# Work orders around the norms and first feed-forward units, one pass for a double norm, a bias by accumulating DMA, and activation tables loaded ahead, in a two-block transformer kernel

## The chip, the cores and the metric

The kernel runs on one core of one Trainium2 chip. The metric is the device time of one execution in microseconds (us); lower is better.

## The reference, cut to what matters

256 tokens of width 1024 pass through two blocks. The first has two layers (a gated linear recurrence, then stick-breaking attention), each followed by a SwiGLU feed-forward, and ends in a norm. The second begins with another norm of that result, so two norms stand back to back.

```python
def rms_norm(x, g):
    return x * lax.rsqrt(jnp.mean(x * x, axis=-1, keepdims=True) + 1e-6) * g

def swiglu_ffn(x, w_in, w_out):                # w_in 1024 x 5632, w_out 2816 x 1024
    gu = x @ w_in
    return (jax.nn.silu(gu[..., :2816]) * gu[..., 2816:]) @ w_out

h = h + rg_lru_block(rms_norm(h, mix_norm[0]), ...)        # ends in y @ w_out + b_out
h = h + swiglu_ffn(rms_norm(h, ffn_norm[0]), ...)
h = h + stick_breaking_attention(rms_norm(h, mix_norm[1]), ...)
h = h + swiglu_ffn(rms_norm(h, ffn_norm[1]), ...)
h = rms_norm(h, final_norm)                                # end of the first block
proj = rmsnorm(h, norm_gain) @ w_in_2                      # start of the second, 24 chunks of 256 columns
# ... q and k head norms, block attention, a gated recurrence, two gated branches, w_out_2, a last gate
```

## The kernel before, in words

**Chunks.** All weights (133 chunks of 128 x 2048 float32, 1 MB each) stream through the core once, in one fixed order. SyncE's queue loads a chunk into one of two `raw` buffers. ScalarE copies it, rounded, to `whi` (L971), VectorE subtracts to get the rest, `wlo` (L1442), and TensorE forms each product as three matmuls (hi by hi, lo by hi, hi by lo; L448 to L457 and L501 to L503). `whi` and `wlo` are rings of four chunks. `split(c)` converts chunk c; it waits for the chunk to land and for TensorE to be done with chunk c - 4. `ahead(c)` is `split(c + 3)`. The load of chunk c + 2 waits for VectorE's half of `split(c)`, so a late split makes the load after next late.

**Order.** There is no scheduler. Each engine runs the list of instructions that its block of the program writes out, in that order, and the engines meet at semaphores. A piece of work that waits holds up everything behind it on its engine.

**Stages.** `STAGES` names them: `rec_a` to `branch_b` and `lru_out` (recurrence), `ffn_in0`, `ffn_out0`, `qkv`, `attn_out`, `ffn_in1`, `ffn_out1`, `mix_in`, `up_a`, `up_b`, `out2`, `ple`, `ple_gate`. At each `..._out` stage the residual `h` is updated half by half (`residual`, L1512). TensorE transposes it (`transposes`, L510; its second half in `late_transposes`), ScalarE multiplies the gain in and rounds to `xhi` (`norm_hi`, L997), VectorE makes `xlo` (`norm_lo`, L1469). The norm's factor is not needed for that: ScalarE squares and sums (`norm_square`, L1007), VectorE adds (`norm_sum`, L1478), ScalarE takes the root (`norm_root`, L1013), VectorE the reciprocal (`norm_factor`, L1485), and the factor is applied to products. For stages whose columns are tokens it goes through `diag` (L1495) and TensorE's `factor_rows` (L518).

**Feed-forward.** A unit is 256 of the 2816 hidden columns, two chunks (inner halves r = 0, 1). When a unit is complete ScalarE takes the sigmoid (L1187), VectorE gates it (`gated`, L1771 and L1776), TensorE transposes it (`gate_transposes`, L649), ScalarE and VectorE split it (`gate_hi`, `gate_lo`). The units stand in 4 banks, two to a unit.

**Attention.** For each of four head groups: `logits`, ScalarE's `log_terms` (exp, then ln), `fail_hi`, VectorE's `neg_log_fail`, TensorE's `suffixes` (L731 and after), `exponents`, `weights` (exp, L1229), `weighted_values`, `outputs`.

**Double norm.** After `ffn_out1` VectorE multiplies `h` by the first factor and the final gain (L1902), ScalarE squares the product (L1341), and `both_factors` gives the factor of both. The head norms of `mix_in` (`head_square`, `head_root`, `head_norm`) and the block attention follow.

**Output bias.** SyncE's queue loads it to all partitions (`bout`), and GpSimd adds it to `h` (L426).

**Tables.** ScalarE's functions come from table sets. Where the next function lies in another set, an ACT_TABLE_LOAD stands in its list.

## Time and profile before

| what | value |
|---|---|
| time, median of 3 runs | 925.23 us (924.8 to 925.44) |
| the profiled execution: its time, and its span | 928.87 us, 927.1 us |
| mean granted clock of TensorE | 0.971 |
| TensorE busy | 855.6 us, 92% |
| VectorE busy | 586.7 us, 63% |
| ScalarE busy | 484.6 us, 52% |
| DMA | 146.17 MB, mean 158 GB/s |

The time is that of the whole execution; the span runs from the first to the last instruction of the profile. A busy TensorE at a granted clock of 0.5 is busy without doing as much as it could, so its idle time and its clock are to be read together.

### The profile page before, as it was taken

The page shows a single profiled execution, that of the slowest core. Times are in us where ns is not written, and L with a number is a line of the kernel's source. Part 1 is how long each engine was busy: PE and PEld are TensorE (multiplying, and loading weights), DVE is VectorE, ACT ScalarE, POOL GpSimd, SP SyncE. Part 2 cuts the span into 40 slices and gives each one's busy share as a digit, 9 for nine tenths or more (in the row PEclk, how much of TensorE's full clock was granted, in tenths as well). Part 3 has the DMA queues.
Part 4 walks back from the last instruction along what each step waited for, and adds up shares of the span by engine and source line. Part 5 has one row for each costly group of instructions (what it writes and reads, how often), then busy time and mean ns, then how long its engine had stood idle before and what let it go on. Part 6 is the DMA issues. An engine that isn't in the chain of part 4 may idle for free.

```text
span 927.1 us, 12198 instructions
## 1 busy us (share of the span) xinstructions
PE 855.6 (92%) x5089; PEld 754.2 (81%) x5089; DVE 586.7 (63%) x703; ACT 484.6 (52%) x555; POOL 18.7 (2%) x14
## 2 busy tenths in 40 slices
PE   4897597999999998999898999999998999999998
PEld 4897475888888898998676888888887999999986
DVE  5788945666653556666436655645465588987864
ACT  5678436444443437676355444443357764557432
POOL 3012000000000000000000000000000000000000
PEclk9899698999999998999999999999999999999999
DMA  8454335655555534444436555556444435443451
GB/s 291 135 171 136 107 120 164 197 184 182 182 182 193 192 116 139 133 137 136 136 109 187 182 182 182 184 196 208 138 144 156 142 106 169 150 136 137 137 182 46
DMA packets 120207, 146.17 MB, mean 158 GB/s; under 512 B 3272, under 2 KB 96984, under 8 KB 120024
## 3 DMA queue, kind: packets, MB, share of 16 engines
q1 hardware_dynamic: 118952, 143.80, 48.0%
q10 hardware_dynamic: 1200, 1.59, 0.5%
q8 instruction: 40, 0.66, 0.3%
q14 instruction: 15, 0.12, 0.0%
HBM read 144.32 MB, written 1.06 MB: 157 GB/s over the span
## 4 chain that ended last, share of the span: by engine, by line
PE 70%; DVE 11%; ACT 11%; DMA 5%; issue 3%; SPq 0%; ACTq 0%; DVEq 0%
PE bank L501 16%; PE bank L503 15%; PE bank L502 15%; DVE wlo L1442 5%; PE bank L448 5%; PE bank L449 5%; PE bank L450 5%; ACT whi L971 4%; DMA raw<-in_lru_w_in 2%; PE bank L854 2%; DMA raw<-in_w_in 1%; PE bank L649 1%; DMA raw<-in_ffn_w_in 1%; PE bank L510 1%; DVE a_rc L1619 1%
## 5 line engine op out<-in xcount | busy, mean ns | idle before, releaser
L1442 DVE TENSOR_TENSOR wlo<-raw,whi 128x2048 fp32r<-128x2048 f32 x133 | 304.7, 2293 | 144.0 <-ACT whi L971 143.7
L971 ACT ACTIVATE whi<-raw 128x2048 fp32r<-128x2048 f32 x133 | 253.4, 1910 | 135.7 <-PE bank L503 44.3
L448 PE MATMUL bank<-xhi,whi 128*128 128x256 f32 x576 | 166.8, 290 | 8.7 <-DVE wlo L1442 5.0
L449 PE MATMUL bank<-xlo,whi 128*128 128x256 f32 x576 | 164.5, 286 | 0.0
L450 PE MATMUL bank<-xhi,wlo 128*128 128x256 f32 x576 | 164.2, 285 | 0.0
L501 PE MATMUL bank<-whi,xhi 128*128 128x512 f32 x384 | 153.6, 400 | 3.8 <-DVE xlo L1469 3.0
L503 PE MATMUL bank<-whi,xlo 128*128 128x512 f32 x384 | 150.7, 392 | 0.0
L502 PE MATMUL bank<-wlo,xhi 128*128 128x512 f32 x384 | 150.6, 392 | 0.0
L448 PEld LDWEIGHTS bank<-xhi,whi 128*128 128x128 f32 x576 | 111.8, 194 | 10.8 <-issue 6.2
L449 PEld LDWEIGHTS bank<-xlo,whi 128*128 128x128 f32 x576 | 112.0, 194 | 0.1
L450 PEld LDWEIGHTS bank<-xhi,wlo 128*128 128x128 f32 x576 | 111.9, 194 | 0.0
L501 PEld LDWEIGHTS bank<-whi,xhi 128*128 128x128 f32 x384 | 73.0, 190 | 19.7 <-issue 5.3
L503 PEld LDWEIGHTS bank<-whi,xlo 128*128 128x128 f32 x384 | 72.8, 190 | 15.7
L502 PEld LDWEIGHTS bank<-wlo,xhi 128*128 128x128 f32 x384 | 72.9, 190 | 14.7 <-issue 0.2
L501 PE MATMUL bank<-whi,a_ghi 128*128 128x512 f32 x176 | 68.9, 391 | 0.0
L503 PE MATMUL bank<-whi,a_glo 128*128 128x512 f32 x176 | 68.5, 389 | 0.0
L502 PE MATMUL bank<-wlo,a_ghi 128*128 128x512 f32 x176 | 68.5, 389 | 0.0
L1187 ACT ACTIVATE a_sg<-bank,stat 128x256 f32<-128x256 f32 x44 | 18.4, 470 | 61.4 <-PE bank L503 61.4
L1168 ACT ACTIVATE a_ghi<-bank 128x512 fp32r<-128x512 f32 x22 | 13.2, 598 | 66.7 <-PE bank L649 66.7
L503 PEld LDWEIGHTS bank<-whi,a_glo 128*128 128x128 f32 x176 | 33.0, 188 | 6.9
L502 PEld LDWEIGHTS bank<-wlo,a_ghi 128*128 128x128 f32 x176 | 33.1, 188 | 6.8
L501 PEld LDWEIGHTS bank<-whi,a_ghi 128*128 128x128 f32 x176 | 33.0, 188 | 6.7
(315 smaller groups left out, 1278.6 us busy)
## 6 DMA issues: line engine op xcount, KB each, us to landing
raw<-in_ffn_w_in SPq DMA_DIRECT2D x88, 512.0 KB, 4.7
raw<-in_w_in SPq DMA_DIRECT2D x24, 1024.0 KB, 5.2
raw<-in_ffn_w_out SPq DMA_DIRECT2D x20, 1024.0 KB, 5.1
raw<-in_attn_w_qkv SPq DMA_DIRECT2D x12, 1024.0 KB, 5.1
raw<-in_lru_w_in SPq DMA_DIRECT2D x8, 1024.0 KB, 6.2
raw<-in_lru_w_out SPq DMA_DIRECT2D x4, 1024.0 KB, 5.2
raw<-in_attn_w_o SPq DMA_DIRECT2D x4, 1024.0 KB, 5.2
raw<-in_w_out SPq DMA_DIRECT2D x4, 1024.0 KB, 5.0
```

What stands on the lines that cost most here:

```text
L448: nc.tensor.matmul(dst, wh, hi, start=start, stop=False, skip_group_check=shared)
L449: nc.tensor.matmul(dst, wh, lo, start=False, stop=False, skip_group_check=shared)
L450: return nc.tensor.matmul(dst, wl, hi, start=False, stop=stop, skip_group_check=shared)
L501: nc.tensor.matmul(dst, hi, wh, start=start, stop=False)
L502: nc.tensor.matmul(dst, hi, wl, start=False, stop=False)
L503: return nc.tensor.matmul(dst, lo, wh, start=False, stop=stop)
L510: last = nc.tensor.transpose(bank[X_BANKS[j]][:, m * S + a * P:m * S + (a + 1) * P], h[:, a, f0:f0 + P], ident)
L854: last = nc.tensor.matmul(dst, k[:, u * P:(u + 1) * P], queries, start=True, stop=True)
L971: nc.scalar.activation(whi[:, c % RING, :], raw[:, c % RAWS, :], ACT.Copy)\
L1168: nc.scalar.activation(ghi[:, q, :], bank[G_BANKS[q % 2]][:, :], ACT.Copy).then_inc(g_hi, 1)
L1187: nc.scalar.activation(sg[:, q % 2, a, :], bank[(b0 + 2 * q + a) % 4][:, 0:S], ACT.Sigmoid, scale=stat[:, 10 * xn + 8 + a:10 * xn + 9 + a] ...
L1442: nc.vector.tensor_tensor(wlo[:, c % RING, :], raw[:, c % RAWS, :], whi[:, c % RING, :].bitcast(F32), ALU.subtract).then_inc(lo_dve, 1)
```

## The change

The feed-forward's chunks are taken in another order for the first two units, the splits and the norm's steps are written elsewhere in the lists, the two norms after `ffn_out1` take their sums of squares in one pass from `h` and from `hg` (`h` times the final gain), the output bias is added by a DMA, and table sets are loaded by an explicit instruction at chosen places.

```diff
+IN_ORDER = OUT_ORDER + tuple((q, r) for q in range(2, FFN_PAIRS) for r in range(2))
+def unit_end(q):
+    return 2 if q == 0 else 2 * q + 1
...
-            sp.dma_start(bout[:, :], bass.AP(t["lru_b_out"].tensor, 0, [[0, P], [1, D]])).then_inc(s_bout, 16)
...
             def output_bias():
-                pool.wait_ge(s_bout, 16)
                 pool.wait_ge(sq_ready, 4)
+                pool.wait_ge(chunk_done, 4)
                 for a in range(2):
-                    nc.gpsimd.tensor_tensor(h[:, a, :], h[:, a, :], bout[:, :], ALU.add).then_inc(bout_in, 1)
+                    nc.gpsimd.dma_start(h[:, a, :], bass.AP(t["lru_b_out"].tensor, 0, [[0, P], [1, D]]),
+                                        accum_op=ALU.add).then_inc(bout_in, 16)
... TensorE, outputs_wide (lru_out, attn_out, out2)
                 part(2, 0, 2)
-                part(3, 0, 2)
+                part(3, 0, 1)
                 if second:
                     second()
+                part(3, 1, 2)
                 part(2, 2, 4)
... TensorE, ffn: over IN_ORDER; p is the chunk's place in ffn_in
+                    if p == 0:
+                        late_transposes(xn, ready, count)
+                    if layer and p == 2:
                         relative_bias()
+                    if p == 4:
+                        gate_transposes(layer, 0)
+                    if p > 4 and p % 2:
+                        gate_transposes(layer, p // 2 - 1)
... TensorE, first_two (qkv, mix_in)
                 columns_part(c0, b0, xhi, xlo, 0, 4, x_lo, 4 * xn)
+                late_transposes(xn, acc_read, 2 * xn)
                 columns_part(c0 + 1, b0 + 1, xhi, xlo, 0, 4, x_lo, 4 * xn)
-                late_transposes(xn, acc_read, 2 * xn)
... TensorE, mix_in
-                2: [lambda: factor_rows(5, 2)],
+                1: [lambda: factor_rows(2)],
... ScalarE
+            nc.scalar.preload_act_table_set("sqrt_and_others")      # the list's first instruction
...
-            def norm_wide(xn, b0):
-                for j in range(4):
-                    norm_hi(xn, j)
-                for c in range(2):
-                    act.wait_ge(banks_read, b0 + 2 * c + 2 + 4)
-                    norm_square(xn, c)
-            norm_wide(1, b0)
-            ahead(c0 + 3)
+            def norm_wide(xn, c0, b0):
+                ahead(c0 + 3)
+                norm_hi(xn, 0)
+                norm_hi(xn, 1)
+                act.wait_ge(banks_read, b0 + 2 + 4)
+                norm_square(xn, 0)
+                act.wait_ge(banks_read, b0 + 4 + 4)
+                norm_square(xn, 1)
+                norm_hi(xn, 2)
+                norm_hi(xn, 3)
... ScalarE, ffn_in
+                for p in range(2 * FFN_PAIRS):
+                    if p == 1:
+                        norm_root(xn)
+                    if p == 3:
+                        sigmoids(0)
+                    if p > 3 and p % 2 == 0:
+                        sigmoids(p // 2 - 1)
+                    split(c0 + p + AHEAD)
... ScalarE, end of ffn_out
-                norm_hi(xn + 1, 2)
-                norm_hi(xn + 1, 3)
                 act.wait_ge(acc_read, 4 * layer + 4)
-                norm_square(xn + 1, 1)
+                if layer:
+                    norm_squares_two(1)
+                    act.wait_ge(ms_ready, 5)
+                    nc.scalar.activation(two[:, :, 6:8], two[:, :, 4:6], ACT.Sqrt, scale=1.0 / D)...
+                else:
+                    norm_square(2, 1)
+                    norm_root(2)
+                nc.scalar.preload_act_table_set("natural_log_exp_and_others")
+                norm_hi(xn + 1, 2)
+                norm_hi(xn + 1, 3)
... ScalarE, attention's last group
             fail_hi(GROUPS - 1)
+            ahead(STAGES["attn_out"][0] + 1)
             weights(GROUPS - 1)
... VectorE, norm_wide; the aheads before it stand before its call
-                ahead(c0 + 1)
-                ahead(c0 + 2)
                 residual_wide(name, 0)
+                ahead(c0 + 3)
                 norm_lo(xn, 0)
                 norm_lo(xn, 1)
                 residual_wide(name, 1)
+                norm_sum(xn)
                 norm_lo(xn, 2)
                 norm_lo(xn, 3)
-                norm_sum(xn)
-                ahead(c0 + 3)
... VectorE, double norm
+                def final_gain(c):
+                    cols = slice(c * WIDE, (c + 1) * WIDE)
+                    for a in range(2):
+                        dve.wait_ge(acc_read, 4 * layer + 2 * c + a + 1)
+                        nc.vector.tensor_tensor(hg[:, a, cols], h[:, a, cols], fgain[:, cols], ALU.mult)...
-                nc.vector.scalar_tensor_tensor(out=h[:, a, :], in0=h[:, a, :], scalar=tok(4, a), in1=fgain[:, :], ...)
+            def final_norm():                                       # in mix_in, c == 5
+                dve.wait_ge(xt_mm, 16)
+                for a in range(2):
+                    nc.vector.tensor_scalar(h[:, a, :], hg[:, a, :], tok(4, a), None, ALU.mult)...
... VectorE, attention's last group
             neg_log_fail(GROUPS - 1)
+            ahead(c0a + 1)
             exponents(GROUPS - 1)
             outputs(GROUPS - 1)
+            ahead(c0a + 2)
```

**Order, VectorE, from the first half of `lru_out`'s residual into `ffn_in0`.** Before, the residual and both pairs of `xlo` come first, and the next split (`wlo`) after them; `a_gt` is the first gated unit.

```order
L1512 TENSOR_TENSOR h<-bank,h 128x512 x2
L1469 SCALAR_TENSOR_TENSOR xlo<-bank,par,xhi 128x256 x4
L1512 TENSOR_TENSOR h<-bank,h 128x512 x2
L1469 SCALAR_TENSOR_TENSOR xlo<-bank,par,xhi 128x256 x4
L1478 TENSOR_TENSOR stat<-stat 128x2
L1442 TENSOR_TENSOR wlo<-raw,whi 128x2048
L1485 RECIPROCAL stat<-stat 128x2
L1442 TENSOR_TENSOR wlo<-raw,whi 128x2048 x2
L1771 SCALAR_TENSOR_TENSOR a_gt<-bank,stat,a_sg 128x256 x2
```

The same place in the changed kernel:

```order
L1548 TENSOR_TENSOR h<-bank,h 128x512 x2
L1478 TENSOR_TENSOR wlo<-raw,whi 128x2048
L1505 SCALAR_TENSOR_TENSOR xlo<-bank,par,xhi 128x256 x4
L1548 TENSOR_TENSOR h<-bank,h 128x512 x2
L1514 TENSOR_TENSOR stat<-stat 128x2
L1505 SCALAR_TENSOR_TENSOR xlo<-bank,par,xhi 128x256 x4
L1478 TENSOR_TENSOR wlo<-raw,whi 128x2048
L1521 RECIPROCAL stat<-stat 128x2
L1478 TENSOR_TENSOR wlo<-raw,whi 128x2048 x2
L1805 SCALAR_TENSOR_TENSOR a_gt<-bank,stat,a_sg 128x256 x2
```

One split (chunk 2 of `ffn_in0`) has moved ahead of the first `xlo`, and four of them instead of three stand ahead of the first gated unit. `attn_out` and `ffn_in1` are written in the same way.

**Order, ScalarE, from the last squares of `ffn_out0` into `qkv` and the first group's `log_terms`.** Before:

```order
L997 ACTIVATE xhi<-bank,par 128x256 x4
L1007 ACTIVATE sq,stat<-h 128x512 x2
L1013 ACT_TABLE_LOAD
L1013 ACTIVATE stat<-stat,small 128x2
L971 ACTIVATE whi<-raw 128x2048
L1246 ACTIVATE a_suffix_r<-const 128x256
L971 ACTIVATE whi<-raw 128x2048 x3
L1215 ACTIVATE a_ee<-a_zz 128x1536
L1216 ACT_TABLE_LOAD
L1216 ACTIVATE a_ee<-a_ee 128x1536
L1219 ACT_TABLE_LOAD
```

In the changed kernel, where no table load follows in the attention stage:

```order
L1017 ACTIVATE sq,stat<-h 128x512 x2
L1029 ACTIVATE stat<-stat,small 128x2
L1244 ACT_TABLE_LOAD
L1006 ACTIVATE xhi<-bank,par 128x256 x4
L980 ACTIVATE whi<-raw 128x2048
L1290 ACTIVATE a_suffix_r<-const 128x256
```

The squares, the root and the table load now come ahead of the second half's `xhi`, and the load of the root's table is gone from here (it stands early in `ffn_out0`).

**Order, ScalarE, from the last `xhi` after `ffn_out1` to the head norms of `mix_in`.** Before:

```order
L1013 ACT_TABLE_LOAD
L1013 ACTIVATE stat<-stat,small 128x2
L1341 ACTIVATE sq,stat<-h 128x1024 x2
L1344 ACTIVATE stat<-stat,small 128x2
L971 ACTIVATE whi<-raw 128x2048 x2
L1277 ACTIVATE a_e_even<-a_mq 128x1024
L971 ACTIVATE whi<-raw 128x2048 x2
L1277 ACTIVATE a_qe<-a_mk 128x1024
L1284 ACT_TABLE_LOAD
L1284 ACTIVATE a_e_even<-bank,small 128x512 x2
L1287 ACT_TABLE_LOAD
L1287 ACTIVATE a_e_even<-a_e_even 128x1024
```

In the changed kernel:

```order
L1017 ACTIVATE sq,stat<-h 128x512 x2
L1017 ACTIVATE sq,stat<-a_hg 128x512 x2
L1239 ACTIVATE stat<-stat 128x2x2
L1244 ACT_TABLE_LOAD
L1006 ACTIVATE xhi<-bank,small 128x256 x4
L980 ACTIVATE whi<-raw 128x2048 x3
L1320 ACTIVATE a_e_even<-a_mq 128x1024
L980 ACTIVATE whi<-raw 128x2048 x2
L1320 ACTIVATE a_qe<-a_mk 128x1024
L1327 ACTIVATE a_e_even<-bank,small 128x512 x2
L1330 ACTIVATE a_e_even<-a_e_even 128x1024
```

The squares of both norms and one root for both stand ahead of the last `xhi`, and the table loads of the head norms are gone. Over its whole list ScalarE has 37 table loads before and 23 in the changed kernel.

## Rows read from the trace of the kernel before

**Rows 1.** The page: busy us (share of the span) and instructions by engine

```profile
PE 855.6 (92%) x5089; PEld 754.2 (81%) x5089; DVE 586.7 (63%) x703; ACT 484.6 (52%) x555; POOL 18.7 (2%) x14
```

**Rows 2.** Waits of TensorE: waiting <- releaser, total us, times, longest us

```profile
PE bank L501 <- DVE a_ylo L1692: 15.9, 2, 8.4
PE bank L649 <- DVE a_gt L1776: 9.9, 2, 5.4
...
PE bank L803 <- DVE a_mk L1932: 3.5, 1, 3.5
...
PE bank L518 <- DVE diag L1495: 3.3, 2, 1.9
...
PE bank L510 <- DVE h L1512: 3.1, 1, 3.1
PE bank L501 <- DVE xlo L1469: 3.0, 2, 1.5
PE bank L448 <- DVE xlo L1469: 2.8, 2, 1.4
```

**Rows 3.** Busy us by stretch; after POOL: granted clock, DMA share, GB/s

```profile
156.40:160.40 4.00, 3.97 (x12) 3.31 (x13) 2.89 (x2) 0.70 (x3) 0.00 (x0) 0.50 0.86 266
...
365.10:372.20 7.10, 7.09 (x34) 7.10 (x35) 6.58 (x7) 4.84 (x3) 0.00 (x0) 0.52 0.25 76
...
460.70:464.90 4.20, 4.15 (x16) 3.42 (x17) 0.88 (x2) 0.88 (x3) 0.00 (x0) 0.59 1.04 345
...
491.80:495.20 3.40, 3.37 (x10) 2.89 (x11) 2.89 (x2) 2.18 (x3) 0.00 (x0) 0.51 0.48 168
...
716.50:720.40 3.90, 3.85 (x21) 3.54 (x22) 3.90 (x11) 0.00 (x0) 0.00 (x0) 0.56 0.80 266
14.00:23.00 9.00, 7.39 (x49) 7.22 (x49) 8.56 (x10) 5.20 (x10) 6.83 (x2) 1.00 0.96 327
...
685.40:690.90 5.50, 5.50 (x49) 5.50 (x48) 4.87 (x5) 4.64 (x3) 0.00 (x0) 1.00 0.52 177
```

**Rows 4.** Timeline, `lru_out` into `ffn_in0`: start, us, engine, [idle before <- releaser]

```profile
126.99 1.29 DVE L1512 TENSOR_TENSOR h<-bank,h 128x512 f32<-128x512 f32 x2 [3.04 <-PE bank L503]
129.90 0.88 DVE L1469 SCALAR_TENSOR_TENSOR xlo<-bank,par,xhi 128x256 fp32r<-128x256 f32 x2 [1.62 <-ACT xhi L997]
142.95 2.29 DVE L1442 TENSOR_TENSOR wlo<-raw,whi 128x2048 fp32r<-128x2048 f32 x1 [1.64 <-ACT whi L971]
150.57 1.91 ACT L971 ACTIVATE whi<-raw 128x2048 fp32r<-128x2048 f32 x1 [4.24 <-DMA raw<-in_ffn_w_in]
```

**Rows 5.** Timeline, ScalarE and TensorE, `ffn_out0` into `qkv`

```profile
334.26 1.57 ACT L997 ACTIVATE xhi<-bank,par 128x256 fp32r<-128x256 f32 x4 [9.10 <-PE bank L510]
338.56 1.90 ACT L971 ACTIVATE whi<-raw 128x2048 fp32r<-128x2048 f32 x1
349.08 1.91 ACT L971 ACTIVATE whi<-raw 128x2048 fp32r<-128x2048 f32 x1 [6.51 <-DMA raw<-in_attn_w_qkv]
357.50 1.28 ACT L1216 ACT_TABLE_LOAD   x1
365.11 0.36 PE L731 MATMUL bank<-a_nlhi,a_suffix_r 128*128 128x256 f32 x1 [3.52 <-DVE a_nllo L1837]
```

**Rows 6.** Timeline, VectorE and TensorE in `attn_out`

```profile
453.29 0.50 PE L501 MATMUL bank<-whi,a_ohi 128*128 128x512 f32 x1 [1.41 <-DVE a_olo L1849]
455.00 4.49 DVE L1442 TENSOR_TENSOR wlo<-raw,whi 128x2048 fp32r<-128x2048 f32 x2 [1.76 <-ACT whi L971]
```

**Rows 7.** Timeline, ScalarE and VectorE, `ffn_out1` into `mix_in`

```profile
670.68 0.64 ACT L1007 ACTIVATE sq<-h 128x512 f32<-128x512 f32 x1
675.66 2.48 DVE L1902 SCALAR_TENSOR_TENSOR h<-h,stat,a_fgain 128x1024 f32<-128x1024 f32 x2
```

**Rows 8.** The chain that ended last, at the start: start us, us, what

```profile
14.09 8.70 DMA raw<-in_lru_w_in
```

More of the change, by code:

```diff
@@ L154, in over @@
             return nc.alloc_sbuf_tensor_at("a_" + name, shape, dt, offset=base + int(kb * 1024))
-        bout = over("bout", 0, [P, D])
         prow = over("prow", 17, [P, 2, P])
@@ L180, in build @@
         fgain = over("fgain", 70, [P, D])
+        hg = over("hg", 62, [P, 2, D])
         qa = over("qa", 0, [P, 2, 2, S])
@@ new lines, in ffn @@
+                for p, (q, r) in enumerate(IN_ORDER):
+                    chunk_ready(None, c0 + p)
+                    if r == 0:
+                        for a in range(2):
+                            pe.wait_ge(banks_read, b0 + 2 * q + a + 1)
+                    for k in range(4):
+                        kk = 4 * r + k
+                        if q == 0 and k % 2 == 0:
+                            pe.wait_ge(x_lo, 4 * xn + kk // 2 + 1)
+                        for a in range(2):
+                            last = product_wide(bank[(b0 + 2 * q + a) % 4][:, :], (c0 + p) % RING, k,
+                                                xhi[:, kk, a * P:(a + 1) * P], xlo[:, kk, a * P:(a + 1) * P],
+                                                kk == 0, kk == DT - 1)
+                    last.then_inc(chunk_done, 1)
+                    if p == 0:
+                        late_transposes(xn, ready, count)
+                    if layer and p == 2:
+                        relative_bias()
+                    if layer and p == 4:
+                        pe.wait_ge(bias_read, 4)
+                    if p == 4:
+                        gate_transposes(layer, 0)
+                    if p > 4 and p % 2:
+                        gate_transposes(layer, p // 2 - 1)
@@ L1164, in ffn, with sigmoids @@
                 c0, _, b0 = STAGES[f"ffn_in{layer}"]
[L1166 to L1181 removed]
+                def sigmoids(q):
+                    act.wait_ge(chunk_done, c0 + unit_end(q) + 5)
                     if q == 0:
@@ L1188, in ffn, with gate_hi @@
                                              scale=stat[:, 10 * xn + 8 + a:10 * xn + 9 + a]).then_inc(sig_ready, 1)
-                c0 = STAGES[f"ffn_out{layer}"][0]
+                def gate_hi(q):
+                    act.wait_ge(gt_mm, FFN_PAIRS * layer + q + 1)
+                    nc.scalar.activation(ghi[:, q, :], bank[G_BANKS[q % 2]][:, :], ACT.Copy).then_inc(g_hi, 1)
+                for p in range(2 * FFN_PAIRS):
[6 more added lines that the diff above has]
+                    split(c0 + p + AHEAD)
+                    if layer and p == 3:
+                        for n in range(4):
+                            act.wait_ge(bias_mm, n + 1)
+                            nc.scalar.activation(pair(bias, n), bank[4 + n][:, :], ACT.Copy)\
+                                .then_inc(bias_read, 1)
+                    if p == 5:
+                        gate_hi(0)
+                    if p > 5 and p % 2 == 0:
+                        gate_hi(p // 2 - 2)
+                c0o = STAGES[f"ffn_out{layer}"][0]
                 for c in range(FFN_PAIRS):
-                    split(c0 + c + AHEAD)
                     if c == 0:
+                        sigmoids(FFN_PAIRS - 1)
+                    split(c0o + c + AHEAD)
+                    if c == 0:
+                        gate_hi(FFN_PAIRS - 2)
+                        nc.scalar.preload_act_table_set("sqrt_and_others")
+                    if c == 2:
                         gate_hi(FFN_PAIRS - 1)
@@ L1523, in norm_wide @@
                 c0 = STAGES[name][0]
-                ahead(c0 + 1)
-                ahead(c0 + 2)
                 residual_wide(name, 0)
+                ahead(c0 + 3)
                 norm_lo(xn, 0)
@@ L1755, in _ @@
             output_lo(3)
-            dve.wait_ge(bout_in, 2)
+            ahead(STAGES["lru_out"][0] + 1)
+            ahead(STAGES["lru_out"][0] + 2)
+            dve.wait_ge(bout_in, 32)
             norm_wide("lru_out", 1)
```

178 lines of the change are left out of this document (82 added, 96 removed).

## The prediction

> **What bounds the kernel now.** I read the page first: TensorE is busy 92% of the span, every other engine 63% or less [rows 1]. So a saving counts only where TensorE waits, or runs at its lower clock. I then read TensorE's waits by releaser [rows 2], the granted clock by stretch [rows 3], and the timeline around each wait [rows 4 to 7]. A chunk takes TensorE 5.5 us (48 matmuls of 256 columns, or 24 of 512; 49 of the first kind stand in the row from 685.40 [rows 3]). The steady stages have no waits; the waits stand where one stage hands over to the next. Where TensorE had stood for more than 3 us the clock was granted at 0.50 to 0.59 for the next 3.4 to 7.1 us, that is, mostly at 1.2 GHz instead of 2.4. After the wait of 1.9 us for `diag` it stayed at 1.00 [rows 2, 3]. A slow stretch costs its length times one minus the clock: 2.0 us (156.4), 3.4 (365.1), 1.7 (460.7), 1.7 (491.8), 1.7 (716.5).
>
> **The change part by part.** The 15.9 us that TensorE waits for `a_ylo` [rows 2] lie in the recurrence, whose lists stay as they are; they are only shifted.
>
> *A, `lru_out` into `ffn_in0`.* Lost now: 5.4 (`a_gt`), 1.5 (`xlo`, the longest of two) and the clock's 2.0, together 8.9 us [rows 2, 3]. Why: chunk 2's split stands after all `xlo` work, so VectorE's half runs at 142.95 to 145.24; the load that it lets go lands at 150.57, 5.3 us later; only behind that chunk's split comes the first unit's gate [rows 4]. In the changed order this split can begin once TensorE is done with `lru_out` chunk 2, at 126.99, where the residual begins [rows 4]. Its load was let go late too, and I place its landing about 1 us behind that. Then 1.9 and 2.3 us of conversion end at 132.2, 13 us earlier than now. The price: the first `xlo` pair is behind it on VectorE and ends 0.9 later, at 133.1, where it now ends at 130.8 [rows 4]. TensorE waits for it: 2.2 us. Behind its late transposes TensorE now finds a chunk that needs only the first half's `xlo`, 5.5 us of work, so the 1.5 us go. Following the lists on: chunk 5's load lands near 150, its split and the sigmoid's table end near 154.5, the gate near 156.1; TensorE wants the banks for chunk 4 at 155.9: 0.3 us. What used to hide the gate (one chunk) is now almost two. Remaining 2.5, gain **6.4**.
>
> *B, `ffn_out0` into `qkv`.* Lost: 1.4 (`xlo`), 3.5 (`a_nllo`) and the clock's 3.4: 8.3 us [rows 2, 3, 5]. The late transposes move 2.8 us forward, behind 24 matmuls instead of 48, and half a chunk of the second column group then covers their conversion. Squares, root and table load (1.3 us) use the time in which ScalarE now idles (9.1 us before 334.26). So chunk 3's split starts near 334.3 instead of 338.56, the load that follows lands about 5 us before 349.08, and `log_terms` loses two table loads of 1.28 us each [rows 5]. `a_nllo` is then ready some 6 us or more sooner, against a wait of 3.5 and TensorE arriving 1.4 sooner. Nothing is left of it: gain **8.3**. The loads taken out in later head groups are worth nothing: TensorE's matmuls cover ScalarE there.
>
> *C, `attn_out` into `ffn_in1`.* Lost: 1.4 (`a_olo`), 3.1 (`h`), 1.7, 1.5, 4.5 (`a_gt`) and 1.7: 13.9 us [rows 2, 3, 6]. Moving the weighted values up by 6 matmuls (1.4 us) covers `a_olo` to 0.2. The wait for `h` is VectorE's two splits from 455.00, 4.49 us ahead of the residual [rows 6]; one is now done before `exponents`, in idle time. The other still waits for ScalarE, behind its two DMA issues. I get the residual 2.0 us after TensorE asks for it: less than 3.1, and short enough to keep the clock. Then `xlo` behind a split, 0.4 (the residual was late anyway). The gate is hidden as in A, and `relative_bias` adds cover. Remaining 2.6, gain **11.3**.
>
> *D, `ffn_out1` into `mix_in`.* Lost: 1.4 (`xlo`), 1.9 (`diag`), 3.5 (`a_mk`), 1.7: 8.5 us [rows 2, 3]. Added: four products `hg` at 0.65 us each on VectorE (as L1512) and four squares on ScalarE (0.64 each) instead of two long ones; taken off: 2.48 us of scaling `h` ahead of a split [rows 4, 7]. Half of the added work lies inside `ffn_out1`, in idle time. The other half stands between the last residual and `xlo`: 1.3 + 1.3 (products, then the second pair of squares) + about 0.8 of sums and root + 1.3 of table load (B's duration) + `xhi` and `xlo` put `xlo` some 8 us behind TensorE's last chunk, the residual's 1.3 ahead of it included; TensorE has 2.8 + 0.8 + 2.8 us of other work until then. It waits 1.5 us, as now. `diag` is early, and the four table loads of the head norms (5.1 us) plus the split that starts 5 us sooner bring `a_mk` in time. What comes late next is the first block attention's `a_probs`: ScalarE's split of the chunk ahead used to fit into the wait for `a_mk`, now it is due after it, and `moba_max`, exponentials, the next split and `moba_scale` follow in a row: I get 2.3 us of new wait. Remaining 3.8, gain **4.7**.
>
> *E, the start.* The chain runs through a load of 1 MB that takes 8.70 us to land [rows 8], in a stretch where the DMA engines are at share 0.96 and 327 GB/s [rows 3]; split, parameters, convolution and the recurrence follow from its landing. Removed: the bias's 0.5 MB in front of it, 1.6 us at that rate. Added at about 16 us: two DMAs of 0.5 MB, 3.2 us at that rate if they are served ahead of it. No row shows an accumulating DMA. Lower end: they come behind, 1.6 us gained. Upper end: each costs double, as it reads what it adds to, 4.8 us lost. I take all of it ahead at the plain rate, the nearest row: **1.6 lost**. The two table loads taken off ScalarE at the start gain nothing, it waits for that landing anyway.
>
> Sum: 6.4 + 8.3 + 11.3 + 4.7 - 1.6 = 29.1 us. The profiled execution took 928.87 us (span 927.1), 3.6 above the median of 925.23. 928.87 - 29.1 = 899.8; against the median, **896**.
>
> **The rivals.**
>
> *R1, loads are the bound where conversions were.* For: A and C rest on loads landing in 5.3 us, while the one at the start takes 8.70 [rows 8], and at 460.7 the engines are at share 1.04 [rows 3]. Against: the steady stages ask for a chunk every 5.5 us, at a share near 0.5 (0.52 in the row from 685.40 [rows 3]). If two loads of each entry land 3 us late, the gate is too, TensorE stands 3.3 us and the clock falls: (3 + 1.8) x 2, about 10 us back: 906.
>
> *R2, no new waits.* The accumulation comes behind the load (E +1.6 instead of -1.6), and the probabilities are in time: 896 - 3.2 - 2.3, about 890. For: no row shows when GpSimd's DMAs begin to move bytes. Against: a share of 0.96 leaves no room beside the load [rows 3]. The Trainium skill ("DMA: Bandwidth & Descriptors", SWDGE vs HWDGE vs iDMA) says that an accumulating DMA is issued by GpSimd alone and that each engine takes turns between its internal queues. By that rule it doesn't queue behind the load but halves its pace, which is E's loss and against R2; no run here shows it yet.
>
> *R3, the double norm gives nothing.* If ScalarE's two squares, root and table load ahead of `xhi` are later than I make them, TensorE waits more than 3 us at 670 and the clock falls: D's 4.7 go, 901.
>
> *R4, slower than before.* VectorE waits for both accumulations before the first residual at 126.99 [rows 4]. They are issued near 16. To undo 29.1 us and pass 0.2% they must land after about 158 us, 1 MB in 142 us or 7 GB/s, against 327 [rows 3]. Nothing in the rows comes near that.
>
> *R5, no change*: the waits return one stage later, each for the same time. For: a split made early frees nothing if the chunk after it is as late as before. Against: in A, 13 us are gained for a wait of 5.4.
>
> **How the numbers follow.** Forecast (890 to 902) 0.52; R1 0.17; R2 with the faster side of the forecast's unknowns 0.16; R3 0.10; R4 0.03; R5 0.02. The range takes in R1, R2 and R3 and E's bounds (893 and 899): 885 to 906. A difference under 0.2%, 1.9 us, can't be told from no change. Faster 0.95, same 0.02, slower 0.03. The likeliest is 896.
>
> **What would show it.** A: `wlo` of chunk 2 near 130 to 132, a wait of about 2 us for the first `xlo`, none over 1 us for `a_gt`. B: none for `a_nllo`. C: a wait for `h` of about 2 us. D: none for `diag` and `a_mk`, about 1.5 for `xlo`, about 2 for `a_probs`. E: the load of rows 8 landing at 24.4. A mean granted clock above 0.971. The prediction is wrong if waits over 3 us with a low clock behind them stand in the feed-forward entries, or if the start is more than 5 us later.

## The result, and the profile after

The changed kernel takes 894.57 us (median of 4 runs, 893.75 to 897.05), the kernel before 925.01 us beside it. The ratio is 0.9676, with a 95% interval of 0.9656 to 0.9697: 3.2% faster, 30 us. The profiled execution took 894.26 us, its span is 892.5, its mean granted clock 0.982. Forecast were 896 us, with a range of 885 to 906.

The page, busy time by engine, beside [rows 1]:

```profile
PE 842.4 (94%) x5089; PEld 744.5 (83%) x5089; DVE 582.6 (65%) x707; ACT 467.0 (52%) x544; POOL 13.8 (2%) x14
```

TensorE does the same 5089 matmuls in 13 us less of busy time. Fewer of them run at the lower clock: the mean granted clock rose from 0.971 to 0.982. The other 21 us between the two traces are idle time. Its waits, beside [rows 2]:

```profile
PE bank L509 <- DVE a_ylo L1724: 15.5, 2, 8.0
PE bank L456 <- DVE a_rclo L1665: 6.9, 2, 6.1
PE bank L821 <- DVE a_probs L2020: 2.6, 1, 2.6
PE bank L456 <- DVE xlo L1505: 2.3, 1, 2.3
PE bank L509 <- DVE xlo L1505: 2.3, 2, 1.7
PE bank L729 <- DVE a_olo L1923: 2.0, 3, 0.7
PE bank L518 <- DVE h L1548: 0.9, 1, 0.9
```

The waits for `a_gt` (9.9 us), `a_nllo` (3.5), `a_mk` (3.5) and `diag` (3.3) are gone. What is left of the handovers is short: `xlo` three times, `h` once, and a wait for `a_probs` of 2.6 us that was 1.3 before. The wait for `a_rclo`, in the recurrence whose lists were not touched, grew from 3.9 to 6.9 us. It moves by itself: the longer of its two waits is 3.7 to 6.1 us in the ten traces here that have the bias DMAs where the change puts them. And the stretch around it is no longer than before.

**Where the time went, by stage.** One event is taken as a mark in each trace: the first residual of `lru_out`, `ffn_out0`, `ffn_out1` and `out2` on VectorE, and the wait for `a_olo` of the third head group on TensorE. In the timeline of the changed kernel (start, us, engine, what) they are:

```profile
126.91 1.29 DVE L1548 TENSOR_TENSOR h<-bank,h 128x512 f32<-128x512 f32 x2 [3.84 <-PE bank L511]
296.17 0.68 DVE L1548 TENSOR_TENSOR h<-bank,h 128x512 f32<-128x512 f32 x1
413.56 0.48 PE L729 MATMUL bank<-a_qa,a_ka 64*128 64x256 f32 x1 [0.66 <-DVE a_olo L1923]
610.16 0.68 DVE L1548 TENSOR_TENSOR h<-bank,h 128x512 f32<-128x512 f32 x1
855.62 0.69 DVE L1548 TENSOR_TENSOR h<-bank,h 128x512 f32<-128x512 f32 x1 [0.38 <-PE bank L511]
```

In the kernel before the same five stand at 126.99 [rows 4], 304.16, 430.14, 639.14 and 890.25. The kernel before was also profiled once more (see the first experiment); its marks are 126.79, 303.85, 429.84, 638.67 and 887.76. Differences of neighbouring marks, in us:

| stretch (part of the prediction) | before | before, again | changed | gain | forecast |
|---|---|---|---|---|---|
| start to `lru_out` (E) | 126.99 | 126.79 | 126.91 | 0 | -1.6 |
| to `ffn_out0` (A) | 177.17 | 177.06 | 169.26 | 7.9, 7.8 | 6.4 |
| to the third head group (B) | 125.98 | 125.99 | 117.39 | 8.6 | 8.3 |
| to `ffn_out1` (C) | 209.00 | 208.83 | 196.60 | 12.4, 12.2 | 11.3 |
| to `out2` (D) | 251.11 | 249.09 | 245.46 | 5.7, 3.6 | 4.7 |
| to the end | 36.85 | 36.84 | 36.88 | 0 | 0 |
| span | 927.1 | 924.6 | 892.5 | 34.6, 32.1 | 29.1 |

In the two traces of the kernel before, the stretches outside the start and D repeat to 0.2 us. In the kernels run below, those that have the same lists in a stretch repeat to 0.1 us in B, in C and at the end. They do not in A (169.26 to 171.42 in four kernels) and not in D (244.65 to 247.03 in nine). A is not independent of the start: in those four kernels the first mark stands between 124.73 and 126.91, the second between 295.77 and 296.17, so A takes back what the start gains. Start and A are best read as one sum; for it the forecast was 4.8 and the gain 8.0 and 7.7.

Two places in detail. `lru_out` into `ffn_in0`, VectorE and ScalarE of the changed kernel, beside [rows 4]:

```profile
129.17 2.29 DVE L1478 TENSOR_TENSOR wlo<-raw,whi 128x2048 fp32r<-128x2048 f32 x1 [0.97 <-ACT whi L980]
131.38 1.65 DVE L1505 SCALAR_TENSOR_TENSOR xlo<-bank,par,xhi 128x256 fp32r<-128x256 f32 x4
149.84 1.92 ACT L980 ACTIVATE whi<-raw 128x2048 fp32r<-128x2048 f32 x1 [4.45 <-DMA raw<-in_ffn_w_in]
153.06 0.84 ACT L1193 ACTIVATE a_sg<-bank,stat 128x256 f32<-128x256 f32 x2
```

The first sigmoid in the kernel before:

```profile
153.79 0.84 ACT L1187 ACTIVATE a_sg<-bank,stat 128x256 f32<-128x256 f32 x2
```

Chunk 2's `wlo` is at 129.17, 13.8 us earlier than the 142.95 of [rows 4]. The split behind which the first sigmoid stands is at 149.84 against 150.57 there; it is that of chunk 5 now and was that of chunk 4. The first sigmoid is at 153.06 against 153.79. The split of chunk 2 came 13.8 us sooner, the first gate 0.7. That asks for an experiment. `ffn_out1` into `mix_in`, ScalarE and VectorE of the changed kernel, beside [rows 7]:

```profile
639.59 0.21 ACT L1239 ACTIVATE stat<-stat 128x4 f32<-128x4 f32 x1 [0.63 <-DVE stat L1828]
639.82 1.28 ACT L1244 ACT_TABLE_LOAD   x1
641.98 1.66 DVE L1505 SCALAR_TENSOR_TENSOR xlo<-bank,small,xhi 128x256 fp32r<-128x256 f32 x4 [1.46 <-ACT xhi L1006]
```

The four squares, the root and the table load stand ahead of the last `xhi`, and TensorE waits 2.3 us for the `xlo` behind them (forecast: 1.5).

### The profile page after: what moved, and what is told of

Same layout as the page of the kernel before. It is cut to its first block, busy times and chain, and to the rows that moved or that the text cites. A ratio compares the mean times of both kernels' runs of the same rounds, so it can differ in the third digit from the quotient of the medians.

```text
span 892.5 us, 12188 instructions
## 1 busy us (share of the span) xinstructions
PE 842.4 (94%) x5089; PEld 744.5 (83%) x5089; DVE 582.6 (65%) x707; ACT 467.0 (52%) x544; POOL 13.8 (2%) x14
## 4 chain that ended last, share of the span: by engine, by line
PE 76%; DVE 9%; ACT 8%; DMA 4%; issue 3%; SPq 0%; ACTq 0%; DVEq 0%
PE bank L509 15%; PE bank L511 15%; PE bank L510 15%; PE bank L456 6%; PE bank L457 6%; PE bank L458 6%; DVE wlo L1478 4%; ACT whi L980 4%; PE bank L463 2%; PE bank L464 2%; PE bank L465 2%; PE bank L863 2%; DMA raw<-in_ffn_w_in 1%; DMA raw<-in_lru_gate_w 1%; PE bank L658 1%
## 5 line engine op out<-in xcount | busy, mean ns | idle before, releaser
L1805 DVE SCALAR_TENSOR_TENSOR a_gt<-bank,stat,a_sg 128x256 f32<-128x256 f32 x44 | 19.3, 480 | 28.4 <-ACT a_sg L1193 28.4
```

The source lines that it names most:

```text
L1805: marks.append(mark(nc.vector.scalar_tensor_tensor(out=gt[:, q % 2, a, :], in0=bank[(b0 + 2 * q + a) % 4][:, 0:S], scalar=tok(xn, a), in1= ...
```

## Experiments

All ratios are to the kernel before, run on the same chip in the same session (its medians: 926.14 us for the bias and `e_split_late`, 925.87 for `e_gate_late`, `e_gate_early`, `f_mid` and `f_best`, 926.72 for the others). The changed kernel was not run again beside them; its ratio is 0.9676 (0.9656 to 0.9697), from its own session.

### The kernel before, profiled again

> The kernel before, unchanged, profiled once more. Its profiled execution took 928.87 us against a median of 925.23, and my trace differences of 34.6 us start from there, while the medians differ by 30.4. If the 3.6 us are a scatter of single executions, this one comes within 1 us of 925 and its trace shows where they lay. If profiling itself costs the kernel before 3.6 us (and the changed kernel nothing: 894.26 against a median of 894.57), it comes at 928 to 929 again.

It took 926.41 us, span 924.6. Profiling does not cost 3.6 us; the profiled execution that stood at the base of the prediction had a span longer by 2.5 us, 2.0 of it in D (251.11 against 249.09 in the table). There a load of `mix_in` landed later, and TensorE's clock was 0.56 behind the wait for `a_mk` [rows 3]. In the second trace that wait was 3.2 us, and the clock behind it stayed at 1.00:

```profile
714.60:718.60 4.00, 3.98 (x35) 3.83 (x36) 4.00 (x11) 0.00 (x0) 0.00 (x0) 1.00 0.81 260
```

### The output bias: back on SyncE's queue, or let go later

```diff
# e_bias_old
+            sp.dma_start(bout[:, :], bass.AP(t["lru_b_out"].tensor, 0, [[0, P], [1, D]])).then_inc(s_bout, 16)
...
-                    nc.gpsimd.dma_start(h[:, a, :], ..., accum_op=ALU.add).then_inc(bout_in, 16)
+                    nc.gpsimd.tensor_tensor(h[:, a, :], h[:, a, :], bout[:, :], ALU.add).then_inc(bout_in, 1)
# e_bias_late
-                pool.wait_ge(chunk_done, 4)
+                pool.wait_ge(rc_ready, 1)
```

> The changed kernel with the output bias as before: a load of 0.5 MB to all partitions on SyncE's queue ahead of the constants, and GpSimd's add. The prediction has the accumulating DMAs cost 1.6 us net (3.2 of DMA time ahead of the 1 MB load against 1.6 saved), so this would come 1.6 us faster, at 893.0. The trace of the changed kernel speaks against it: its start is 0.8 us earlier than in the trace before, so the rival expects this kernel 0.5 to 1.5 us slower, 895 to 896, with the 1 MB load landing near 22.8 us again instead of 21.7. If the first matmuls of the gates depend on neither, within 0.5 us.

895.28 us (5 runs), ratio 0.9663 (0.9650 to 0.9676).

> The changed kernel with its two accumulating DMAs let go only when the recurrence stage is under way (near 39 us) instead of at 16 us. If they take DMA time from the load of the gates' weights, which lands at 31.3 us in the changed kernel and on which ScalarE waits 1.15 us, that load lands about 3 us earlier and the kernel is 1.1 us faster (893.5), the most that the chain at the start gives before ScalarE's own work is the bound. Rival, the DMAs cost nothing where they are: no change, within 0.4 us. A third way, that the transfer let go at 39 us now collides with the chunk loads of the recurrence: up to 1 us slower.

895.17 us (4 runs), ratio 0.9661 (0.9647 to 0.9674). Neither differs from the changed kernel's 0.9676. The chain of the changed kernel at the start:

```profile
2.61 7.95 DMA raw<-in_lru_w_in
20.95 10.36 DMA raw<-in_lru_gate_w
```

The load of [rows 8] is no longer in the chain: ScalarE splits that chunk at 21.73 instead of 22.81. The next load does carry the accumulation (10.36 us, ScalarE waits 1.15 us for it), and let go late it doesn't: that split starts at 28.92 instead of 31.32. In the kernel with the late DMAs:

```profile
28.92 1.90 ACT L980 ACTIVATE whi<-raw 128x2048 fp32r<-128x2048 f32 x1
```

So the accumulating DMAs share the engines with a load, as the Trainium skill has it ("DMA: Bandwidth & Descriptors", SWDGE vs HWDGE vs iDMA), but mainly with the load after the one that I had named. What it costs can't be seen at the next mark: the first residual stood at 124.7 with the late DMAs, at 126.4 with the old way, and between 124.6 and 126.9 in ten executions that have the DMAs where the change puts them. The start scatters by 2.3 us, more than the whole of E. At an earlier point the order is clear in every trace. The first long wait for `a_ylo` ends at 94.70 and 94.74 in the kernel before and at 94.40 with the bias in the old way. With the DMAs where the change puts them it ends between 92.88 and 93.99 (ten traces), and with the late DMAs at 92.40. By these traces the DMAs gain 0.4 us or more there against the old way (one trace, and the two of the kernel before), and late ones somewhat more (one trace); neither shows in the total time.

### One piece undone at a time: the early split, the order of chunks

```diff
# e_split_late (ScalarE; VectorE alike), in norm_wide
-                ahead(c0 + 3)
                 norm_hi(xn, 0)
...
                 norm_hi(xn, 3)
+                ahead(c0 + 3)
# e_order_old
-IN_ORDER = OUT_ORDER + tuple((q, r) for q in range(2, FFN_PAIRS) for r in range(2))
+IN_ORDER = tuple((q, r) for q in range(FFN_PAIRS) for r in range(2))
```

> The changed kernel with one piece undone: in lru_out and attn_out the split of chunk 2 of the following feed-forward stands behind all of the norm's work again, on ScalarE and VectorE, while the order of the chunks stays changed. By the prediction's reason for parts A and C (the early split is what makes the first gated unit early; chunk 2's wlo at 145 instead of 131), waits for a_gt of 3 us and more with a low clock behind them come back in both feed-forward entries: 4 to 6 us each, 902 to 906. Rival: the order of chunks alone hides the gate, and the early split only makes the first xlo late (1.7 and 0.6 us of wait): then this kernel is within 1 us, or up to 2 us faster.

897.86 us (4 runs), ratio 0.9693 (0.9677 to 0.9708). This interval overlaps that of the changed kernel, but not those of the two bias kernels of the same session (0.9663 and 0.9661), which have the split early.

> The changed kernel with the feed-forward's chunks in their natural order (unit 0's two chunks, then unit 1's), the gate of a unit taken behind its second chunk, and the early split kept. The prediction's parts A and C say what the new order is for: behind the late transposes stands a chunk that needs only the first half's xlo (1.5 us of wait in each entry go), and almost two chunks instead of one hide the first gate. If so: two waits for xlo of about 1.5 us come back (+3.0) and, with only one chunk of cover, a_gt waits of up to 5 us with the low clock behind them in each entry (up to +7 each); 900 to 912. Rival: the early split alone brings the gate in time, and this kernel has only the xlo waits: 897 to 898. Second rival: the order is worth nothing, within 1 us of 894.9.

898.96 us (4 runs), ratio 0.9699 (0.9683 to 0.9716).

> The changed kernel with both undone, natural order of chunks and the split of chunk 2 behind the norm's work. It is the way of the kernel before in lru_out/ffn_in0 and attn_out/ffn_in1, except for the places of the squares, of the weighted values and of the relative bias. The prediction's A and C together are 17.7 us, of which about 3 belong to the weighted values' place and the wait for h: so +13 to +16, 908 to 911, with a_gt waits of 4.5 to 5.4 us and the clock near 0.5 behind each. The late split alone cost about 3 us. Rival, the two pieces overlap (either one alone does most of it): then the late split and the old order each cost little alone and only both together the full amount. If the gain came from somewhere else, under +5.

894.64 us (4 runs), ratio 0.9655 (0.9639 to 0.9671). The first two go some way as expected: a late split alone brings a wait for `a_gt` of 3.9 us back in `ffn_in0` (only 1.0 in `ffn_in1`), and the old order with the early split has `xlo` waits of 5.8 us in all. The third is a plain miss. With **both** undone, which I had put at 908 to 911, the kernel is as fast as the changed one. By stretch, A was 170.36 and C 197.89, against 169.26 and 196.60. So neither the early split nor the order is what brought most of A's and C's gain. What these three kernels still have from the change is that the gates stand later in the lists. The first unit's sigmoid and gating come one split later and its transposes two chunks later; for the other units the transposes come one chunk later, and what reads them later too.

### The gate at its old place, with a late and with an early split

Both have the natural order of chunks; `relative_bias` is back at its old place too.

```diff
# e_gate_late, e_gate_early (TensorE; the sigmoids, gated, gate_hi and gate_lo go back too)
-                    if p == 4:
-                        gate_transposes(layer, 0)
-                    if p > 4 and p % 2:
-                        gate_transposes(layer, p // 2 - 1)
+                    if p > 1 and p % 2 == 0:
+                        gate_transposes(layer, p // 2 - 1)
```

> Natural order of chunks, split of chunk 2 behind the norm's work (as in the run that undid both, 894.6 us), and in addition the gate of a unit taken one chunk earlier, as in the kernel before: its transposes on TensorE behind the first chunk of the next unit, its sigmoid behind the split of that chunk's ring place. My theory after the runs so far: what removed the waits for a_gt is the place of the gate in TensorE's list (two chunks of cover instead of one), not the early split. Then the two waits come back whole, 5.4 and 4.5 us with a slow stretch of 2.0 and 1.7 behind them, less the 1.4 that this kernel's sibling waits: +11 to +12, 905 to 907. Rival: the gain of parts A and C came from the other moves in these stages (squares earlier, root a split later, weighted values earlier), and the gate's place gives little: under +4.

902.07 us (4 runs), ratio 0.9741 (0.9723 to 0.9758). The waits for `a_gt` are back:

```profile
PE bank L658 <- DVE a_gt L1802: 6.2, 2, 4.1
PE bank L509 <- DVE xlo L1497: 3.0, 2, 1.5
```

> The same, natural order and the gate at its old place, but with the split of chunk 2 early, as in the changed kernel. The prediction took the early split for what brings the gate forward by some 13 us. In the lists the sigmoid now stands behind the split that the trace of the changed kernel shows at 143.5 us instead of 149.8. If that is right the gate is ready near 149.5, before TensorE asks for it: no wait for a_gt, and only the xlo waits of the run with the old order and the early split (899.0): 898 to 900; either piece alone would then do most of the work. If instead the gate's place is the only thing that counts, the waits for a_gt come back here too, and this is 905 to 912, with the xlo waits on top.

899.48 us (4 runs), ratio 0.9712 (0.9695 to 0.9730). No wait for `a_gt`, but four for `xlo`:

```profile
PE bank L509 <- DVE xlo L1497: 5.4, 4, 1.8
```

ScalarE's first sigmoid in the timeline of the kernel with the late split:

```profile
148.25 1.28 ACT L1191 ACT_TABLE_LOAD   x1
149.55 0.84 ACT L1191 ACTIVATE a_sg<-bank,stat 128x256 f32<-128x256 f32 x2
```

And in that of the kernel with the early one:

```profile
145.72 1.28 ACT L1191 ACT_TABLE_LOAD   x1
147.02 0.84 ACT L1191 ACTIVATE a_sg<-bank,stat 128x256 f32<-128x256 f32 x2
```

In the kernel with the early split it does what the prediction claimed: the sigmoid stands behind a split that has run early, and the gate is ready. In the changed kernel it stands one split further back (149.84), and the early split is used up. Later gate and early split are two answers to one wait, and whichever comes second is worth little. The four combinations in natural order: the ratio, then from the trace the mark of `ffn_out0` and the length of C in us:

| natural order of chunks | gate at its old place | gate later |
|---|---|---|
| split late | 0.9741; 300.67, 200.14 | 0.9655; 294.94, 197.89 |
| split early | 0.9712; 297.55, 198.37 | 0.9699; 298.31, 198.36 |

The later gate is worth 0.9% (8 us) alone, and mark and C together give the same 8.0 us. The early split is worth 0.3% (2.7 us) alone. Mark and C give 4.9, but its trace took 2.1 us more in D, whose lists are the same, with slow stretches there that the trace of the late split did not have. Behind the later gate the early split costs 0.4% (3.8 us by mark and C), by the `xlo` waits in front of which it stands and a slow stretch behind the first of them (granted clock 0.59). In the new order the early split is of use again (0.9693 without; 0.9676, 0.9663 and 0.9661 with), since unit 0 is complete only with its third chunk. The expectation of 905 to 907 for the late split was still too high: A lost 5.3 us against its sibling (175.70 to 170.36), C only 2.3 (200.14 to 197.89). C keeps 8.7 to 8.9 of its gain with all three pieces undone. What is left of the change there is the weighted values moved up and a split moved ahead of `exponents` (the waits of 1.4 for `a_olo` [rows 6] and of 3.1 for `h` [rows 2] are at most 0.3 and 0.9), and the squares, which now run in ScalarE's idle time ahead of the late `xhi` instead of between it and the next split. I didn't test these one by one, so how the 8.7 us divide among them is not shown.

### Table sets

```diff
# e_no_preload
-            nc.scalar.preload_act_table_set(...)      # every one of them
```

> The changed kernel without the explicit table loads: the compiler puts a load where a function from another set comes next, as in the kernel before, so ln and exp come from two sets and the 14 loads of 1.28 us each return, but at the places of the changed lists. By the prediction loads matter only where ScalarE is on the path: one of log_terms in the first head group (B, whose a_nllo had 6 us to spare against 2 or 3 loads of 1.28) and those of the head norms (about 5 us of slack): +0 to +1.5 us, 895 to 896. Rival: the explicit loads are what brings a_nllo and a_mk in time: waits for a_nllo of 1 to 3 us and for a_mk of 2 to 5 us come back, with the low clock where they pass 3 us: +5 to +9 us, 900 to 904.

896.03 us (5 runs), ratio 0.9656 (0.9638 to 0.9673): no difference that can be told, with 37 table loads in ScalarE's list again. `a_nllo` is waited for 0.6 us, `a_mk` not at all. From the timeline of this kernel, behind all four loads of the head norms, ScalarE's split, VectorE's `a_mk` and TensorE's score matmuls:

```profile
677.36 1.90 ACT L980 ACTIVATE whi<-raw 128x2048 fp32r<-128x2048 f32 x1
681.50 1.28 DVE L1992 SCALAR_TENSOR_TENSOR a_mk<-a_mk,par,a_qe 128x1024 f32<-128x1024 f32 x1
682.87 0.49 PE L812 MATMUL bank<-a_mk,a_mq 64*128 64x256 f32 x2
```

`a_mk` is ready at 682.78, 0.1 us before TensorE comes at 682.87. Of B's 8.6 us 0.9 go (118.27 instead of 117.39). The Trainium skill gives a switch of sets 2.66 us with its drain ("ScalarE: Activation LUTs", What ACT_TABLE_LOAD costs); here the load takes 1.28 us and the next activation follows within 0.02, so the 14 loads are 18 us of ScalarE's time, and what they are worth in the end is not above what this measurement can tell.

### The double norm as before

```diff
# e_double_old
-                if layer:
-                    norm_squares_two(1)
...
-                nc.scalar.preload_act_table_set("natural_log_exp_and_others")
+                norm_square(xn + 1, 1)
+                norm_root(xn + 1)
+                if not layer:
+                    nc.scalar.preload_act_table_set("natural_log_exp_and_others")
                 norm_hi(xn + 1, 2)
... the second norm's scaling of h, squares and root behind the first split of mix_in, as in the kernel before
```

> The changed kernel with the double norm as before: first norm's factor, h scaled by it and the final gain in two instructions of 2.48 us, two squares of the scaled h over 1024 columns, a second root, and diag for the pair behind them. The prediction's part D: the wait for diag of 1.9 us returns and part of a_mk's, the wait for xlo gets shorter (now 2.3, with squares and root in front of it): +1 to +4 us, 896 to 899. Rival R3, the one pass gives nothing: within 0.5 us, or faster by up to 2.3 us, since xlo is no longer late at all. If ScalarE's later table load delays the head norms: a_mk of 3 us and more with the low clock, +5 to +7 us.

892.03 us (4 runs), ratio 0.9627 (0.9613 to 0.9642). It is faster than the changed kernel, by 2.5 us in the medians and 4.5 in the ratios, whose intervals don't overlap; by stretch, D is 243.07 against 245.46. Only the side that went with R3 had held that open. ScalarE, and VectorE, where `xlo` was late:

```profile
636.56 0.30 ACT L1029 ACTIVATE stat<-stat,small 128x2 f32<-128x2 f32 x1 [0.23 <-DVE stat L1515]
636.97 1.57 ACT L1006 ACTIVATE xhi<-bank,small 128x256 fp32r<-128x256 f32 x4
637.92 1.66 DVE L1506 SCALAR_TENSOR_TENSOR xlo<-bank,small,xhi 128x256 fp32r<-128x256 f32 x4 [0.86 <-ACT xhi L1006]
```

The first norm's root takes 0.30 us where its table is there already, and can stand ahead of `xhi`; `diag` and `xlo` are then both in time, without a wait. The one pass puts two more squares and a table load there, for a `diag` that is early anyway. And `a_mk` is in time in both kernels that undo half of what was meant to help it. Without the explicit loads (`e_no_preload`) the chunks of `mix_in` are early: ScalarE's split stands 0.8 us behind TensorE's first head sum. Here they are late (that split at 661.67, 3.9 us behind it), but the head norms have no table loads. Each half covers the 3.2 to 3.5 us by itself.

### The split moved by two places, and everything put together

```diff
# f_mid (ScalarE, then VectorE)
-                ahead(c0 + 3)
                 norm_hi(xn, 0)
                 norm_hi(xn, 1)
+                ahead(c0 + 3)
...
                 residual_wide(name, 0)
-                ahead(c0 + 3)
                 norm_lo(xn, 0)
                 norm_lo(xn, 1)
                 residual_wide(name, 1)
+                ahead(c0 + 3)
# f_best: f_mid, e_double_old, and on ScalarE
-                if c == 7:
-                    moba_exp(0)
                 if c == 8:
+                    moba_exp(0)
                     decay_exp()
```

> The changed kernel with the early split moved a little: on ScalarE behind the first half's xhi, on VectorE behind the second half of the residual, still ahead of the second half's xhi and xlo. VectorE idles there for 3.7 us (before) between the residual and xlo, and a split takes 2.3. The first xlo is then as early as in the kernel before, its waits (1.7 to 2.4 us in lru_out, 0.6 in attn_out, sometimes with a slow stretch behind them) go, and the split is still one ahead, so no gate waits: -2 to -3.5 us, 891.5 to 893. Rival: the split now lies before the second xlo and the late transposes find it late, or the gate waits 3 us as with the late split: 895 to 899.

892.29 us (5 runs), ratio 0.9635 (0.9618 to 0.9652). VectorE in `lru_out`:

```profile
131.11 0.88 DVE L1505 SCALAR_TENSOR_TENSOR xlo<-bank,par,xhi 128x256 fp32r<-128x256 f32 x2 [0.94 <-ACT xhi L1006]
131.90 1.28 DVE L1548 TENSOR_TENSOR h<-bank,h 128x512 f32<-128x512 f32 x2
133.10 2.28 DVE L1478 TENSOR_TENSOR wlo<-raw,whi 128x2048 fp32r<-128x2048 f32 x1
```

The split fills time in which VectorE stood idle; the two first `xlo` waits are gone, and `a_gt` is waited for 0.4 us. A is 1.6 us shorter than in the changed kernel and C 0.5.

> The changed kernel with three things put right: the split moved as in the run before this one, the double norm as in the kernel before (its root ahead of xhi and its table already loaded, 892.0 us alone), and the exponentials of the first block attention placed behind the split of the next chunk on ScalarE, so that VectorE's split and moba_scale are not held up. If each removes what the trace shows beside it: -2.5 to -3 (double norm), -2.0 to -3.5 (first xlo), -2.6 to -4 (a_probs and what stands behind it), 885 to 888. Rival: a wait removed late in the program returns at the next meeting of the engines, above all a_probs, whose exponentials then start up to 2 us later: 889 to 891.

885.53 us (4 runs), ratio 0.9561 (0.9544 to 0.9578): 4.4% below the kernel before, and 1.2% (the intervals don't touch) below the changed one. The handovers in its list of waits:

```profile
PE bank L729 <- DVE a_olo L1916: 2.0, 3, 0.7
PE bank L518 <- DVE h L1548: 0.9, 1, 0.9
PE bank L821 <- DVE a_probs L2022: 0.6, 1, 0.6
```

Its stretches are 126.08, 167.65, 117.40, 196.10, 240.10 and 36.87. Against the changed kernel: A 1.6, C 0.5, D 5.4. The wait for `a_probs` fell from 2.6 to 0.6: VectorE's split no longer waits for a `whi` that stands behind the exponentials. The three things were not run apart from each other here, beyond `f_mid` and `e_double_old`.

## Why the prediction was right, point by point

- **Sum.** 29.1 was forecast, the medians differ by 30.4, the two traces by 34.6. The traces' 34.6 holds 2 us that the profiled execution of before had lost; against its repeat it is 32.1.
- **A, right in size, wrong in its reason.** Forecast 6.4, measured 7.8 to 7.9. The steps "13 us earlier than now" and a first `xlo` that is 2.2 late were seen (129.17; 1.7 us), and so was "0.3 us" for the banks (0.5). But the reason given, chunk 2's late split, is not what carries A: the first gate came 0.7 us sooner, and with the split and the order both undone the gain stays. The prediction's own working had the gate only at 156.1; the step that carries A is the one in a half-sentence, "What used to hide the gate (one chunk) is now almost two". The size holds some luck: with the same lists A was up to 171.42 long, a gain of 5.7, depending on where the start's mark and the clock behind the first `xlo` fell.
- **B, right.** 8.3 forecast, 8.6 measured, nothing left. That the table loads have a part in it was overstated: they are 0.9 of it.
- **C, right in size.** 11.3 forecast, 12.2 to 12.4 measured. The wait for `h` was over-sized: 2.0 forecast, 0.9 measured. The term for the gate (4.5 and 1.7) belongs to the later gate only in part: with the gate at its old place the wait is 2.1 us with the late split and none with the early one, and the clock behind it stays at 1.00. The rest went with other pieces of the change there, which were not tested apart.
- **D, right in sum, wrong in sign for its core.** 4.7 forecast, 3.6 to 5.7 measured. `diag` and `a_mk` went and `a_probs` came (2.3 forecast, 2.6 measured), `xlo` was 2.3 instead of 1.5. But the one pass costs about 2.5 us; by the traces the gain is that of the root ahead of `xhi` and of either of two ways to an early `a_mk`. I had taken one package as one cause. The 1.7 us put down for the clock behind `a_mk` stood in only one of the two traces of the kernel before.
- **E, wrong.** 1.6 lost was forecast, the mark moved by 0.1, and no variant of the bias differs in time. The step that failed is "all of it ahead" of the load of [rows 8]. Taking the bias's 0.5 MB away did bring that load's split forward, from 22.8 and 23.2 to 21.7, but the 3.2 us of accumulation were not in front of it: they meet the load after it. At the wait for `a_ylo` the start is 0.7 to 1.9 us earlier than before, where 1.6 later was forecast; at the mark itself it scatters by more than the term.
- **Rivals.** R1 did not come: the load that ScalarE waits for has landed at 149.84, near the 150 of the forecast, and TensorE never stands 3.3 us at the entries. R2's half on `a_probs` is refuted by 2.6 us, its half on the bias has the right sign at the wait for `a_ylo` and is lost in the scatter behind it. R3 did not come as a time (901), nor its mechanism (a wait of more than 3 us), but its claim that the one pass gives nothing holds. R4 is refuted. R5 holds only in that the early split gives nothing behind a later gate.

## What to carry to other kernels

Where a change makes one wait go in two ways at once, undo both before crediting either: here three pieces looked necessary, two of them were answers to the same wait, and the second cost time. A piece of work that is moved ahead to be early should go into a hole of its engine, not in front of what the next engine waits for; moving one split by two places gave 2.3 us in the medians. And with repeatable kernels, cut the span at marks and compare the stretches. Here three of six repeat to 0.1 us where the total scatters by 2; profile kernels that are alike in a stretch to learn which ones do.

## What the runs showed that was not expected

The clock behind a wait is not a function of the wait alone. TensorE waits 2.6 us for `a_probs` in the changed kernel and in the one with order and split undone. The next 4 us of the changed kernel (stretch, length, busy us by engine, then granted clock, DMA share, GB/s):

```profile
697.60:701.60 4.00, 4.00 (x24) 4.00 (x25) 1.81 (x7) 3.94 (x4) 0.00 (x0) 0.64 0.75 256
```

And of the one with both undone:

```profile
697.60:701.60 4.00, 4.00 (x33) 3.55 (x32) 1.77 (x7) 3.94 (x4) 0.00 (x0) 1.00 0.77 256
```

24 matmuls against 33 in the same 4 us, from the same instructions after the same wait. Eleven of the kernels run here have this wait of 2.6 us; seven show 0.50 to 0.64 behind it, four show 1.00. Nine of them also wait 2.0 to 2.3 us for `xlo` at the entry of `mix_in`; four show 0.57 to 0.68 behind that, five show 1.00. In `lru_out` a wait of 1.8 us had 0.57 behind it (early split, gate at its old place), one of 2.65 us had 1.00 (old double norm). The prediction's reading of [rows 3], that the waits of more than 3 us are the ones that cost the clock, was too simple in both directions. In these traces slow stretches stood behind waits as short as 1.8 us, each costing 1.3 to 2 us (4 us times one minus the granted clock), and the wait of 3.2 us for `a_mk` had none behind it in the repeated trace of the kernel before. That is most of the scatter in D: of the nine kernels with both waits it is 244.7 to 244.8 us long in the three with neither slow stretch, 245.5 to 246.9 in the three with one, and 246.7 to 247.0 in the three with both. What decides between the two is open.
